# Sixteen of the first block's input products as eight pairs of seven half-size products, in a stretch of their own

## The chip, the cores and the metric

One NeuronCore of a Trainium2 chip (trn2) runs the whole program in one launch. The metric is the device time of that launch in microseconds (us). The engines are TensorE (PE in the rows, its weight loads PEld), VectorE (DVE), ScalarE (ACT), GpSimd (POOL) and the queue of SyncE (SP), which issues most loads.

## The reference, cut to what matters

Two transformer-like blocks run one after the other on 1024 tokens of width 1024. The change is in the first block, where the normalised input (and a context of 256 tokens) is multiplied by one wide matrix and cut into ten parts:

```python
u_l, v_l, q_l, k_l, vv_l, r_l, af_l, ab_l, ga_l, gb_l = jnp.split(h_lat @ w_in, offs, axis=-1)
ql, kl, vl, lfl, lbl = _gla_heads(q_l, k_l, vv_l, af_l, ab_l, w_alpha_f, b_alpha_f, w_alpha_b, b_alpha_b)
o_lf, _ = _gla_scan(ql, kl, vl, lfl, s_cf)
o_lb, _ = _gla_scan(fl(ql), fl(kl), fl(vl), fl(lbl), s_cb)
b_lat = _gla_out(o_lf + fl(o_lb), r_l, gla_norm_g, h_lat.dtype)
a_lat = _chunk_mlp(u_l, v_l, ...)
y = jax.nn.sigmoid(ga) * (a_lat @ w_branch_a) + jax.nn.sigmoid(gb) * (b_lat @ w_branch_b)
```

`u`, `v`, `r`, `ga`, `gb`, `vv` are 1024 wide, `q` and `k` 512. `u` and `r` are needed only after the scan. The rest of the first block, its SwiGLU and the whole second block are untouched.

## The kernel before, in words

**Products.** Every float32 operand is kept as two float32r parts, high and low, and a product is high by high, input low by weight high, and input high by weight low: three matmuls for each of the eight slices of 128 input rows. One weight tile is 128 output columns. A fill job is one tile by 512 tokens, 8 x 3 = 24 matmuls of 128x512 into one PSUM bank (`products_pe`, L319 to L321). A job of kind "rows" (`rows_pe`, L420 to L422) turns it round: 128 tokens are the stationary operand, and the four weight tiles of a group move as 512 columns, so the job needs all four tiles. It waits for the high and low parts of the group's last tile, which are made in order.

**Weights.** `weight_order` lists all tiles. SP loads each tile raw into one of NS = 2 buffers (`weights_sp`, L289; the next load into a buffer waits until the low part of the tile before in it is made), ACT makes the high part (`weights_act`, L271), DVE the low part (`weights_dve`, L278). The parts lie in NW = 4 places (`WH`, `WL`; `place`), and for some tiles in four more (`XWH`, `XWL`, `in_second`), which share memory with `RES`. A high part waits until its place is free (`before_in_place`). When each is made is written into the job that stands at that point of every engine's program: `p.make = n` has ACT and DVE make all tiles below n ahead of what they do for that job, and SP issue loads up to n + 2.

**Stage 1** (`stage1`, about 95 to 320 us) runs 39 jobs: the last tile of `k` (3, one of them the 256 tokens of context), `q` (8), `vv` as rows in two groups of four tiles (20) and half of `v` as rows (8). Beside each job stands one unit of the decays (24 in all: `decay_pe` L904, `decay_act` L919 to L923, `decay_second_dve` L947 to L954) and one dot product for the modulation (32, `mod_dve` L959, with a 512 KB load each).

**Stage 2** (`stage2`, about 320 to 659 us) runs the scan in 20 slots, the two directions in turn, with 40 jobs as fillers, two to a slot: the other half of `v` (8), `u` (16) and `r` (16). A slot is, on PE, two jobs, then the phases 3, 4, 5 of slot n (turn the keys L1263, outputs L1276 and L1278, state L1287), then phase 2 of slot n + 1 (L1251, L1255). DVE, in its program, follows with the states of slot n (L1239), phase 6 (L1191), phase 2 of slot n + 1 (L1209 to L1225) and phase 1 of slot n + 2 (L1197 to L1204), and only then reaches the next job's weights. Steps 0 and 1 of a direction are context slots with no output products, and from step 6 on a slot also adds the other direction's part. The stage's other engines begin when every engine's last signal of stage 1 has come (`gone`).

**Stage 3** (`stage3`, from 659 us) has 32 jobs, `ga` (16) and `gb` (16), with the work on `u`, `v`, `r` and the scan's output behind them (`behind`). Its ACT and DVE programs begin when stage 2 has ended on all engines.

Which engine waits for what around a "rows" job, and where its weights are made, is in these lines:

```python
def fill_act(p):
    if p.make:
        weights_act(p.make)
    ACW.wait_ge(*p.mm)
```

Of the kernel before, what the change touches and what calls it, by code (L numbers as in the profile page):

```python
# [7 lines left out]
F = mybir.dt.float32  # L8
# [7 lines left out]
TC = 256  # L16
NF = 22
EPS = 1e-6
NW = 4
# [44 lines left out]
class Job:  # L64


    def __init__(self, i, name, m, col, n, half, x, ready, bank):
# [7 lines left out]
        self.make, self.group, self.chunk = None, None, None  # L75
# [29 lines left out]
CHUNKS = (8, 12)  # L105

# [19 lines left out]
def program(nc, D, out):  # L126
# [56 lines left out]
    T2H, T2L, T3H, T3L = placed(*(([128, 4, 512], R, n) for n in ("t2h", "t2l", "t3h", "t3l")))  # L183
    XWH, XWL = placed(([128, NW, 1024], R, "xwh"), ([128, NW, 1024], R, "xwl"))
# [53 lines left out]
    def in_second(i):  # L238

        return 5 <= i < 9 or 13 <= i < 17 or 21 <= i < 25  # L240

    def place(i):
        return (i - 1) % NW
# [6 lines left out]

    def before_in_place(i):

        if i < NW or 5 <= i < 9:
            return []
        return [used[i - 2 * NW if 9 <= i < 29 else i - NW]]
# [135 lines left out]
    def plan_rows(jobs, name, group, banks, dst, key, chunks):  # L391

        i = tile_of[(name, 4 * group + 3)]
        for chunk, half, c, x, ready in chunks:
            p = Job(i, name, group, c, 512, half, x, ready, banks[len(jobs) % len(banks)])
            p.bank_free = bank_free[p.bank]
            p.mm = mm.at(more("mm"))
# [5 lines left out]
        for j in range(4):  # L403
            used[i - j] = jobs[-1].mm

    def rows_pe(p):
# [7 lines left out]
        PEW.wait_ge(*w_lo.at(p.i + 1))  # L414
        for k in range(8):
# [96 lines left out]
    def fill_sp(p):  # L512
        if p.make:
            weights_sp(p.make + NS)
# [5 lines left out]
    def stage0():  # L520
# [5 lines left out]
        XC = alloc(p0, [128, 8, TC], F, "xc")  # L526
        mrow = alloc(p0, [2, 2048], F, "mrow")
# [325 lines left out]
    def stage1(parts, xt, low_rank, gone):  # L853

        (al_hi, al_lo, wal_hi, wal_lo, cm_in, cb_silu), done = low_rank
        p1 = ExitStack()
        LG = alloc(p1, [128, 2, 2, 512], F, "lg")
        DG = alloc(p1, [128, 2, 512], F, "dg")
        aw = alloc(p1, [128, 1024], F, "aw")
        aw_in = sig("in", "aw")  # L860
        d_mm, d_abs, d_ln = sig("pe", "decay_product"), sig("ac", "decay_abs"), sig("ac", "decay_log")
# [8 lines left out]
        for group in range(2):  # L870
            plan_rows(jobs, "vv", group, banks, dV, "v", of_context + token_chunks(2, (0, 1)))
        plan_rows(jobs, "v", 0, banks, dVm, "vm", token_chunks(0, (0, 1)))
        for p in jobs:
            p.make = None
        for j, upto in ((0, 7), (2, 8), (3, 9), (5, 10), (7, 11), (8, 12), (9, 13), (11, 14), (13, 15), (15, 16), (17, 17),
# [30 lines left out]
        def pe_():  # L906
            for what, j in steps:
                if what == "fill":
                    fill_pe(jobs[j], None)
                elif j < 24:  # L910
                    decay_pe(j)
# [2901 lines left out]
```

## Time and profile before

| | us |
|---|---|
| median of three runs | 3247.93 (3247.49 to 3249.04) |
| the profiled execution, its own time | 3249.49 |
| its span, first to last instruction | 3248.2 |
| PE busy | 3175.4 (98%) |
| DVE, ACT, POOL busy | 1892.3, 1408.1, 393.3 |
| mean granted TensorE clock | 0.993 |

In a row, the first number is the start or the busy time, and the bracket at the end is the idle time before with what ended it. A matmul's record covers its whole latency, so two records overlap: what a matmul costs in a stream is the distance from one start to the next. A float32 matmul has two records, a float32r matmul one (L1251 issues four float32 matmuls and shows eight records; a fill job issues 24 and shows 24). The granted clock is a share of 2.4 GHz; 0.50 is the lower level, 1.2 GHz.

### The profile page before, as it was taken

The numbers are of one execution on the slowest core, as the hardware profiler recorded it, in microseconds if no ns is written. First come the engines' busy times: TensorE is split into PE (matmuls) and PEld (weight loads), VectorE is DVE, ScalarE is ACT, GpSimd is POOL, SyncE is SP. The second block draws the span as 40 slices with busy tenths as digits, with TensorE's granted clock in tenths as the row PEclk, the third lists the DMA queues.
The fourth block names the chain that finished last, engine by engine and source line by source line (L and its number), as shares of the span: only waits on it lengthen the run. The fifth ranks groups of instructions, "written<-read, shape, count | busy, mean of one in ns | idle before, by whom it ended". The sixth has DMA issues, their size and how long they took to land.

```text
span 3248.2 us, 38749 instructions
## 1 busy us (share of the span) xinstructions
PE 3175.4 (98%) x14558; PEld 2584.2 (80%) x14558; DVE 1892.3 (58%) x3053; ACT 1408.1 (43%) x2336; POOL 393.3 (12%) x625
## 2 busy tenths in 40 slices
PE   6999999999999999999999999999899999999998
PEld 4888788888888878888888887877667888888886
DVE  5562344565334487777444546656686787776443
ACT  4791232254333243333233376575576443333221
POOL 1111000012000200000010200112221200001011
PEclk8999999999999999999999999999999999999999
DMA  5564544456542323334763444355876432336652
GB/s 231 180 223 157 166 149 155 127 209 217 177 143 101 132 98 111 112 115 144 242 197 95 144 136 137 124 172 170 178 114 154 149 123 104 123 104 216 207 189 68
DMA packets 228489, 495.13 MB, mean 152 GB/s; under 512 B 21712, under 2 KB 84816, under 8 KB 226768
## 3 DMA queue, kind: packets, MB, share of 16 engines
q1 hardware_dynamic: 146688, 298.11, 29.2%
q0 software_dynamic: 81616, 194.55, 19.0%
q8 instruction: 117, 1.92, 0.3%
q14 instruction: 68, 0.56, 0.1%
HBM read 353.63 MB, written 138.94 MB: 152 GB/s over the span
## 4 chain that ended last, share of the span: by engine, by line
PE 85%; DVE 7%; ACT 3%; DMA 2%; issue 2%; POOL 0%; SPq 0%; DVEq 0%; POOLq 0%; ACTq 0%
PE p L2273 12%; PE p L2275 12%; PE p L2274 12%; PE p L319 12%; PE p L321 11%; PE p L320 11%; PE p L420 2%; PE p L421 2%; PE p L422 2%; PE p L3341 1%; PE p L1287 1%; PE p L3327 1%; PE p L1276 1%; DMA s_qs<-d_q2l 1%; DMA s_ad<-i_ada 1%
## 5 line engine op out<-in xcount | busy, mean ns | idle before, releaser
L319 PE MATMUL p<-s_xh,s_wh 128*128 128x512 f32 x1936 | 767.1, 396 | 9.8 <-DVE s_tmp L476 6.0
L321 PE MATMUL p<-s_xh,s_wl 128*128 128x512 f32 x1936 | 754.9, 390 | 0.0
L320 PE MATMUL p<-s_xl,s_wh 128*128 128x512 f32 x1936 | 754.3, 390 | 0.0
L2273 PE MATMUL p<-s_xh,s_wh 128*128 128x512 f32 x1152 | 449.7, 390 | 1.5 <-DVE s_wl L2522 1.3
L2275 PE MATMUL p<-s_xh,s_wl 128*128 128x512 f32 x1152 | 448.3, 389 | 0.0
L2274 PE MATMUL p<-s_xl,s_wh 128*128 128x512 f32 x1152 | 448.2, 389 | 0.0
L319 PEld LDWEIGHTS p<-s_xh,s_wh 128*128 128x128 f32 x1936 | 363.6, 188 | 96.6 <-issue 11.1
L321 PEld LDWEIGHTS p<-s_xh,s_wl 128*128 128x128 f32 x1936 | 363.5, 188 | 76.8
L320 PEld LDWEIGHTS p<-s_xl,s_wh 128*128 128x128 f32 x1936 | 363.8, 188 | 74.3 <-issue 1.9
L278 DVE TENSOR_TENSOR s_wl<-s_ws,s_wh 128x1024 fp32r<-128x1024 f32 x143 | 176.7, 1247 | 208.6 <-ACT s_wh L271 208.3
L464 ACT ACTIVATE s_tmp<-p 128x512 f32<-128x512 f32 (+1 forms) x157 | 93.0, 593 | 429.3 <-PE p L321 340.8
L2273 PEld LDWEIGHTS p<-s_xh,s_wh 128*128 128x128 f32 x1152 | 216.2, 188 | 48.8 <-issue 3.6
L2274 PEld LDWEIGHTS p<-s_xl,s_wh 128*128 128x128 f32 x1152 | 216.2, 188 | 45.2 <-issue 0.5
L2275 PEld LDWEIGHTS p<-s_xh,s_wl 128*128 128x128 f32 x1152 | 216.2, 188 | 44.9
L271 ACT ACTIVATE s_wh<-s_ws 128x1024 fp32r<-128x1024 f32 x143 | 148.3, 1050 | 56.0 <-PE p L321 38.6
L2419 ACT ACTIVATE s_wh<-s_ws 128x512 fp32r<-128x512 f32 x148 | 91.9, 625 | 144.5 <-PE p L2275 111.2
L2419 ACT ACTIVATE s_wh<-s_qb 128x512 fp32r<-128x512 f32 x140 | 87.2, 625 | 119.3 <-PE p L2275 109.8
L2643 POOL DMA_DIRECT2D d_h<-s_fhl x80 | 42.6, 533 | 742.7 <-DVE s_fhl L2527 734.3
L2522 DVE TENSOR_TENSOR s_wl<-s_ws,s_wh 128x512 fp32r<-128x512 f32 x148 | 106.3, 731 | 32.6 <-ACT s_wh L2419 32.3
L2522 DVE TENSOR_TENSOR s_wl<-s_qb,s_wh 128x512 fp32r<-128x512 f32 x140 | 100.1, 724 | 40.0 <-ACT s_wh L2419 39.8
L2425 ACT ACTIVATE s_fhl<-s_rb 128x512 fp32r<-128x512 f32 x80 | 50.7, 633 | 151.5 <-DVE s_rb L2567 132.8
L2419 ACT ACTIVATE s_wh<-s_s 128x512 fp32r<-128x512 f32 x80 | 50.0, 625 | 134.7 <-DVE s_s L2512 123.2
(437 smaller groups left out, 5497.4 us busy)
## 6 DMA issues: line engine op xcount, KB each, us to landing
d_h<-s_fhl POOLq DMA_DIRECT2D x80, 512.0 KB, 3.0
s_ws<-i_Wf SPq DMA_DIRECT2D x48, 512.0 KB, 4.2
s_qb<-i_Wf SPq DMA_DIRECT2D x40, 512.0 KB, 4.2
s_qb<-i_Wf SPq DMA_DIRECT2D x80, 256.0 KB, 2.9
s_ws<-i_Wf SPq DMA_DIRECT2D x80, 256.0 KB, 2.8
s_aw<-i_adaT SPq DMA_DIRECT2D x32, 512.0 KB, 3.7
s_xh<-d_h POOLq DMA_DIRECT2D x16, 1024.0 KB, 12.3
s_xl<-d_h POOLq DMA_DIRECT2D x16, 1024.0 KB, 15.4
```

Of the source, the lines that this page charges most:

```text
L271: ac.activation(high_of(i), raw_weights(i)[0], ACT.Copy).then_inc(*w_hi.up())
L278: dv.tensor_tensor(low_of(i), raw_weights(i)[0], high_of(i).bitcast(F), ALU.subtract).then_inc(*w_lo.up())
L319: pe.matmul(o, wh, H[:, k, c:c + n], start=(k == 0), stop=False)
L320: pe.matmul(o, wh, L[:, k, c:c + n], start=False, stop=False)
L321: last = pe.matmul(o, wl, H[:, k, c:c + n], start=False, stop=(k == 7))
L420: pe.matmul(o, xh, wh, start=(k == 0), stop=False)
L464: ac.activation(o, ps, ACT.Copy, scale=p.scale).then_inc(*evA.up())
L2273: pe.matmul(o, wh[:, c], H[:, k, :], start=(start and k == 0), stop=False)
L2274: pe.matmul(o, wh[:, c], L[:, k, :], start=False, stop=False)
L2275: x = pe.matmul(o, wl[:, c], H[:, k, :], start=False, stop=(stop and k == 3))
L2419: ac.activation(half_tile(u.slot)[0], u.src, ACT.Copy).then_inc(*u_hi.up())
L2522: dv.tensor_tensor(l, u.src, h.bitcast(F), ALU.subtract).then_inc(*u_lo.up())
```

## The change

**Seven products in place of eight.** For two weight tiles and all tokens, an output of 256 columns by 1024 tokens over 1024 input rows is cut into halves in all three sizes. Seven half-size products P1 to P7 replace eight. Each is 4 slices x 3 = 12 matmuls of 128x512 (`unit_pe`). Before, such a pair took 4 jobs x 24 = 96 matmuls, now 7 x 12 = 84. It is done for the 8 tiles of `u` and the 8 of `r`: 8 pairs. Four combined inputs are summed once (40 elementwise operations of 128x512, 28 on POOL and 12 on DVE) and split (16 on ACT, 16 on DVE). For each pair, DVE makes four combinations of the raw weights (`fold_dve`) and seven low parts, ACT seven high parts, two copies of one PSUM bank into another as the start of a later sum (`pair_act`, P1 and P6), one copy of P5 into `HELD`, and two outputs; DVE adds `HELD` to the other two. SP loads 1 MB of raw weights per pair, two pairs deep. Two more matmuls, whose result is not used, write the two banks first.

```diff
+SEVEN = ("P1", "P5", "P6", "P2", "P7", "P3", "P4")
+SEVEN_TILES = [(n, m) for n in ("u", "r") for m in range(0, 8, 2)]
+SEVEN_FIRST = 17
...
+        def unit_pe(u, fresh):
...
+            for k in range(4):
...
+                pe.matmul(o, wh[:, c], H[:, k, :], start=(fresh and k == 0), stop=False, skip_group_check=not fresh)
+                pe.matmul(o, wh[:, c], L[:, k, :], start=False, stop=False, skip_group_check=not fresh)
+                x = pe.matmul(o, wl[:, c], H[:, k, :], start=False, stop=(k == 3), skip_group_check=not fresh)
...
+            for u in units:
+                pair_act(pairs[u.n], u.name)
+                high_act(u.i + 7)
+                tail_weights(weights_act, u)
```

**Where it stands.** The 8 pairs are a stretch at the end of stage 1. The order of all other jobs moves: stage 1 has 31 (no `v`), stage 2 has 22 (three tiles of `ga`, 6 jobs, then `v` in two groups of 8), three in slot 0 and one in each later slot, and stage 3 has 26. The places of the weights are renumbered, and only `vv`'s first group still uses `XWH`. The decays' 24 units go in 12 pairs, one every second job, with Abs, Exp and Ln each done for both (`decay_act`). Half the dot products (16) stay beside the jobs and two go with each pair.

```diff
-    for n in ("v", "u", "r", "ga", "gb"):
-        order += [(n, m) for m in range(8)]
+    order += [("ga", m) for m in range(3)] + [("v", m) for m in range(8)]
+    order += [("ga", m) for m in range(3, 8)] + [("gb", m) for m in range(8)]
...
-        return 5 <= i < 9 or 13 <= i < 17 or 21 <= i < 25
+        return 9 <= i < 13
...
-        items = [("u", m, False, "plain", dU, "u", 1.0, TC) for m in range(8)] + [("r", m, False, "plain", dR, "r", 1.0, TC) for m in range(8)]
+        items = [("ga", m, False, "plain", dGA, "ga", 1.0, TC) for m in range(3)]
...
+        plan_rows(jobs, "v", 0, banks, dVm, "vm", token_chunks(0, (0, 1)), (0, 1, 2, 3))
         plan_rows(jobs, "v", 1, banks, dVm, "vm", token_chunks(0, (0, 1)))
-        for j in range(4):
-            jobs[2 * j].make = 26 + j
...
+        for j, upto in ((0, 21), (2, 22), (4, 23), (6, 24), (14, 28)):
+            jobs[j].make = upto
...
-        gaps = [len(jobs) * n // 20 for n in range(21)]
+        gaps = [0] + [len(jobs) - 20 + n for n in range(1, 21)]
```

So tile 23 is the last of `v`'s first group (jobs 6 to 13), and tiles 24 to 27 are its second (jobs 14 to 21); tile 28 is the first of stage 3.

**In pieces.** The last job of `vv`'s second group and of `v`'s first group is done one weight tile at a time, each piece 24 matmuls with 128 moving columns. Each piece signals on its own, and a tile's place counts as used up when its piece is done (`used`):

```diff
+        for a in p.pieces:
+            for k in range(8):
+                xh, xl = H[:, k, p.col:p.col + 128], L[:, k, p.col:p.col + 128]
+                wh, wl = WHg[:, a, k * 128:k * 128 + 128], WLg[:, a, k * 128:k * 128 + 128]
+                pe.matmul(o[:, a, :], xh, wh, start=(k == 0), stop=False)
+                pe.matmul(o[:, a, :], xl, wh, start=False, stop=False)
+                last = pe.matmul(o[:, a, :], xh, wl, start=False, stop=(k == 7))
+            last.then_inc(*mm.up())
```

**Stage 3** drops six filler jobs and its work behind them is drawn together: two `norm` steps behind job 14, the second half's `mix` from 16, `fetch` behind 22 and `first` behind 23.

## Rows read from the trace of the kernel before

**Rows 1.** The page: busy time of the engines, share of the span, instructions.
```profile
PE 3175.4 (98%) x14558; PEld 2584.2 (80%) x14558; DVE 1892.3 (58%) x3053; ACT 1408.1 (43%) x2336; POOL 393.3 (12%) x625
```
**Rows 2.** By stretch: length; busy PE, PEld, DVE, ACT, POOL; granted clock, DMA.
```profile
95.00:320.00 225.00, 225.00 (x1009) 186.80 (x1008) 116.14 (x160) 145.69 (x183) 35.08 (x65) 1.00 0.59 195
...
332.00:338.00 6.00, 4.22 (x11) 3.24 (x12) 2.58 (x6) 0.68 (x3) 0.54 (x1) 0.56 0.70 218
...
382.00:660.00 278.00, 278.00 (x1408) 235.33 (x1407) 127.90 (x257) 75.19 (x135) 21.63 (x40) 1.00 0.44 140
```
**Rows 3.** Timeline of PE, slots 0 and 1 of the scan: start, us.
```profile
327.20 0.39 PE L420 MATMUL p<-s_xwh,s_xh 128*128 128x512 f32 x1
...
330.38 0.39 PE L422 MATMUL p<-s_xwl,s_xh 128*128 128x512 f32 x1
333.09 1.12 PE L1263 MATMUL p<-s_ident,s_ks 128*128 128x128 f32 x4 [2.33 <-DVE s_ks L1211]
...
338.12 0.99 PE L420 MATMUL p<-s_xwh,s_xh 128*128 128x512 f32 x1
...
339.67 0.40 PE L420 MATMUL p<-s_xwh,s_xh 128*128 128x512 f32 x1
...
349.91 0.60 PE L1263 MATMUL p<-s_ident,s_ks 128*128 128x128 f32 x4
...
352.89 0.58 PE L420 MATMUL p<-s_xwh,s_xh 128*128 128x512 f32 x1
```
**Rows 4.** Timeline of PE: float32r with 256 moving columns, first and last of 25.
```profile
105.38 0.28 PE L319 MATMUL p<-s_ch,s_wh 128*128 128x256 f32 x1
...
108.25 0.28 PE L904 MATMUL p<-s_al,s_wal 128*128 128x256 f32 x1
```
**Rows 5.** Timeline of PE: eight records that move one column, each with its load.
```profile
62.72 0.95 PE L641 MATMUL p<-s_ones,s_ad 128*128 128x1 f32 x8
63.52 0.49 PE L319 MATMUL p<-s_xh,s_wh 128*128 128x512 f32 x1
```
**Rows 6.** Timeline of PE where slots 4 and 12 and stage 3 begin.
```profile
382.83 0.50 PE L319 MATMUL p<-s_xh,s_wh 128*128 128x512 f32 x1
...
513.26 1.05 PE L1251 MATMUL p<-s_gq,s_ki 128*128 128x128 f32 x8
514.25 0.68 PE L1255 MATMUL p<-s_gq,s_ks 128*64 128x64 f32 x8
514.86 0.50 PE L319 MATMUL p<-s_xh,s_wh 128*128 128x512 f32 x1
...
658.89 0.58 PE L319 MATMUL p<-s_xh,s_wh 128*128 128x512 f32 x1
```
**Rows 7.** Timeline of DVE at the same three places.
```profile
386.54 0.15 DVE L1204 TENSOR_TENSOR s_ep<-s_eb 128x4 f32<-128x4 f32 x1
...
519.36 1.22 DVE L278 TENSOR_TENSOR s_wl<-s_ws,s_wh 128x1024 fp32r<-128x1024 f32 x1
...
661.51 1.23 DVE L278 TENSOR_TENSOR s_wl<-s_ws,s_wh 128x1024 fp32r<-128x1024 f32 x1 [1.36 <-ACT s_wh L271]
```
**Rows 8.** Timeline of ACT at slot 12 and where stage 3 begins.
```profile
515.58 1.05 ACT L271 ACTIVATE s_wh<-s_ws 128x1024 fp32r<-128x1024 f32 x1
...
660.32 1.06 ACT L271 ACTIVATE s_wh<-s_ws 128x1024 fp32r<-128x1024 f32 x1 [5.58 <-DVE s_S L1239]
```
**Rows 9.** DMA issues, 330 to 660 us: count, KB, median us to landing.
```profile
s_ws<-i_Wr SPq DMA_DIRECT2D x8, 512.0 KB, 3.9
```
**Rows 10.** Groups by line: count | busy us, mean ns of one | idle before.
```profile
L1164 ACT ACTIVATE s_e<-s_gb 128x512 f32<-128x512 f32 x16 | 10.0, 625 | 0.0
...
L2527 DVE TENSOR_TENSOR s_fhl<-s_rb,s_fhl 128x512 fp32r<-128x512 f32 x33 | 22.5, 683 | 0.7 <-ACT s_fhl L2425 0.7
...
L1633 POOL TENSOR_TENSOR s_acc<-s_acc,s_tmp 128x512 f32<-128x512 f32 x49 | 63.8, 1302 | 336.4 <-ACT s_tmp L1626 336.2
...
L959 DVE CUSTOM_DVE_ANT_0 s_aw<-s_aw,s_cb 128x1024 f32<-128x1024 f32 x32 | 39.1, 1222 | 50.1 <-DMA s_aw<-i_adaT 50.1
```

More of the change, by code:

```diff
@@ L396, in plan_rows @@
             p.bank_free = bank_free[p.bank]
+            p.pieces = []
+            if chunk == chunks[-1][0]:
+                p.pieces = pieces
+                for a in pieces[:-1]:
+                    used[i - 3 + a] = mm.at(more("mm"))
             p.mm = mm.at(more("mm"))
@@ L402, in plan_rows @@
             jobs.append(p)
-        for j in range(4):
-            used[i - j] = jobs[-1].mm
+        for a in range(4):
+            if a not in pieces[:-1]:
+                used[i - 3 + a] = jobs[-1].mm
     def rows_pe(p):
@@ L513, in fill_sp @@
         if p.make:
[L514 removed]
+            weights_sp(min(p.make + NS, p.top))
     def ended(*outs):
@@ L879, in stage1 @@
-        steps = beside(len(jobs), [("side", s) for s in range(33)], 1)
-        dbank = [list(bank_free[4]), list(bank_free[5])]
+        decays = [(d, h, part) for d in range(2) for h in range(4) for part in range(3)]
+        steps, n_dots = [], 0
+        for j in range(31):
+            steps += [("before", j), ("fill", j)]
+            if j % 2 == 0 and j <= 24:
+                steps.append(("decay", j // 2))
+            if j % 2 or j == 20:
+                steps.append(("dot", n_dots))
+                n_dots += 1
@@ new lines, in stage1, with load_pair_sp @@
+        dots_of_pair = [list(range(n_dots + 16 * n // n_pairs, n_dots + 16 * (n + 1) // n_pairs)) for n in range(n_pairs)]
+        assert n_dots == 16
+        def load_pair_sp(p):
+            x = RAW[p.n % 2]
+            if p.n >= 2:
+                SPW.wait_ge(*pairs[p.n - 2].units["P4"].lo)
+            elif p.n == 1:
+                SPW.wait_ge(*d_mm.at(24))
+                SPW.wait_ge(*d_scan.at(24))
+                for s in d_out:
+                    SPW.wait_ge(*s.at(12))
+            else:
+                SPW.wait_ge(*w_lo.at(SEVEN_FIRST))
+            for i in range(2):
+                sp.dma_start(x[:, 1024 * i:1024 * i + 1024], D["W" + p.name][p.m + i]).then_inc(*raw[2 * (p.n % 2) + i].up())
@@ L941, in decay_second_dve @@
         def decay_second_dve(u):
-            d, h, part = units[u]
+            d, h, part = decays[u]
             n = parts(True)[part][2]
@@ new lines, in dve_, with store_pool @@
+            for i in range(7):
+                low_dve(i)
+            for u in units:
+                p = pairs[u.n]
+                pair_dve(p, u.name)
+                fold_dve(u.i + 8)
+                low_dve(u.i + 7)
+                if u.name in ("P5", "P2") and dots_of_pair[p.n]:
+                    mod_dve(dots_of_pair[p.n].pop(0))
+                tail_weights(weights_dve, u)
+            mods_end_dve()
+        def store_pool(p, name):
+            o = p.outs[name]
+            POW.wait_ge(*o.ev)
+            dst = dU if p.name == "u" else dR
+            po.dma_start(dst[o.m][:, 512 * o.h:512 * o.h + 512], TMP[:, o.slot, :]).then_inc(*stored[o.slot].up())
@@ L997, in stage1 @@
+            for p in pairs:
+                for name in ("P2", "P7", "P3", "P4"):
+                    store_pool(p, name)
         sp_()
```

398 lines of the change are left out of this document (326 added, 72 removed).

## The prediction

> **What bounds the kernel now.** I read the page first: PE is busy for 3175.4 of 3248.2 us [rows 1], so the sum is first a sum of PE's time. The stretches come next. In those where the change works, PE has no idle time at all in 95 to 320 us and in 382 to 660 us, at the full granted clock, with DVE and ACT about half busy [rows 2]. What ends a wait there is therefore not an average load of DVE or ACT but the moment at which they reach one instruction of their programs. The only stop near the change is in the scan's first slot, where PE waits 2.33 us for DVE [rows 3]. All sums below are against the profiled execution (3249.5 us, its span 3248.2); it stands 1.6 us above the median of the runs, and the forecast is given against that median.
>
> **What is saved.** Fifteen matmuls of 512 columns start from 327.20 to 330.38, 14 distances, so one costs 0.227 us [rows 3]. Eight pairs go from 96 to 84 matmuls: 96 fewer in all, 21.8 us. The two matmuls of no use give back 0.5. Everything else on the list of jobs is only moved: 39 + 40 + 32 = 111 jobs before, 31 + 22 + 26 + 32 after.
>
> **The pieces.** Two jobs of 24 matmuls become two of 96 with 128 moving columns: 48 x 0.227 = 10.9 us go and 192 of an unknown price p come. No float32r matmul in the trace moves 128 columns. With 256 columns the distance is (108.25 - 105.38) / 24 = 0.120 us [rows 4]. When only one column moves behind a load of 128 columns it is (63.52 - 62.72) / 8 = 0.100 [rows 5]: a load with nothing to hide it is no cheaper. So halving the 256 columns can take off little, and 0.100 is the lower end. The upper end is a float32 matmul of 128 columns, which takes two records, (514.25 - 513.26) / 8 x 2 = 0.248 [rows 6]. I take 0.120, because that row has the same number type, the same load and one record. The pieces then cost 23.0 - 10.9 = +12.1 us, with ends at +8.3 and +36.7. What they are for, an earlier free place, can't be used in stage 2: in ACT's program the weights of job 14 stand behind its wait for the whole of job 13.
>
> The Trainium skill, "TensorE: Matmul & The Clock Gate", section Back-to-back issue gap, gives about 81 ns a matmul for sustained streams of 128 columns and about 131 ns for 512. For 512 columns this trace says 0.227, so the section does not fit this kernel; by its 81 ns the pieces would cost 15.6 - 10.9 = +4.7 us as an estimate.
>
> **Waits that the change adds in stage 2.** PE itself keeps up: a slot with one job is 5.4 us + 5.5 of scan, and DVE's chain ends 3.9 us after a job starts (382.83 to 386.69) [rows 6, 7]. The weights don't. A place is free only when the tile four before it has been used, and a "rows" job needs all four tiles.
> - Job 6 needs tile 23, whose place is used until job 5 ends, and whose making is written at job 6. ACT and DVE come to it after their part of slot 3. DVE's part ends at 386.69, and a low part takes 1.22 us [rows 7]: 387.9 against 382.83 [rows 6], PE waits **5.1 us**. Nothing covers it; job 6 is next on PE.
> - Job 14 needs tiles 24 to 27, and all four are made there. The same place in the trace before is slot 12: PE starts its job at 514.86 [rows 6], ACT a high part at 515.58 (1.05 us) [rows 8], DVE a low part at 519.36, so until 520.58 [rows 7]. Two raw tiles are in the buffers, so the second low part is done at 521.8. The third load can be issued only when the first low part is made: 520.6 + 3.9 to land [rows 9] + 1.05 + 1.22 = 526.8. The fourth: 521.8 + 3.9 = 525.7, + 1.05 + 1.22 = 528.0. PE waits **13.2 us**. Behind SP's waits for these loads stand the next slot's loads; they have a slot (12.7 us with job and scan) and are not late.
> - Tile 28 is the first of stage 3, and its place is used until job 21 ends. ACT starts a high part at 660.32, when stage 2 has ended everywhere [rows 8], and DVE's low part ends at 662.74 [rows 7], against PE's 658.89 [rows 6]: **3.9 us**.
> - In slot 0 there are now three jobs ahead of the first turn of keys where there was one and another one: 5.4 us more cover than the 2.33 us wait [rows 3]. That wait goes.
>
> **The clock.** After those 2.33 us idle the granted clock is 0.56 on average from 332 to 338 [rows 2], so mostly the lower level, 1.2 GHz. From the turn of keys to the next fill PE takes 338.12 - 333.09 = 5.03 us, and 352.89 - 349.91 = 2.98 in the next slot; three fills then take 1.55 against 0.68 [rows 3]. A fall so costs 2.9 us. It goes with the wait in slot 0 (-2.3 - 2.9 = -5.2), and comes with the waits of jobs 6 and 14 (+5.8). At stage 3's wait I leave it out and count it in the range.
>
> **What lies beside.** In the seven-product stretch one product is 12 x 0.227 = 2.7 us of PE, a pair 19.1. Per pair ACT has seven high parts and five copies, 12 x 0.625 = 7.5 us, and DVE seven low parts, four sums and two outputs, 13 x 0.683, and two dot products of 1.222, together 11.3 us [rows 10]. Weights are made seven products ahead. The copy that P6 needs has P5's 2.7 us to hide in, and P4's wait for DVE has P3's. All of it counted at nothing; if the chains slip, PE stops once or twice a pair. POOL's 28 sums of 1.302 us are 36 us [rows 10] beside ten jobs of 5.4; they hold stores back by under two jobs, with four buffers. The decays in pairs save ACT some table loads, and nobody waits for ACT there, since PE has no idle time [rows 2]: nothing gained. The first pair's weights: places are freed piece by piece in `vv`'s last job, and there the making does stand ahead of ACT's wait for that job; counted at nothing. Stage 3's tighter list has at most two DVE steps more in one job; nothing, with up to 2 us in the range.
>
> **Sum:** -21.8 + 0.5 + 12.1 - 5.2 + 5.1 + 13.2 + 3.9 + 5.8 = **+13.6 us**. Against the median of 3247.9 that is 3261.5 us. The saving is real, but it is spent on pieces and on weights that come too late.
>
> **Rivals.**
> 1. *Pieces at two records.* If float32r with 128 columns takes what float32 does, +36.7 in place of +12.1: 3286. For it: nothing in this trace runs float32r under 256 columns, and both float32 rows have two records. Against: nothing else makes a float32r matmul take a second record. 0.24.
> 2. *Faster: the weights are in time.* If engines reach the weights of jobs 6, 14 and 28 under cover of the scan, the 22.2 us of waits and 5.8 of clock go: -14.4, 3233.5. Its place is the end of slot 11. It decides once the added waits with their clock are under about 8 us in all, for then the sum is 6.5 us below before. Against: two of the four loads can't be issued before DVE's first low parts, and one load is 3.9 us. 0.09.
> 3. *Cheap pieces.* If loads of a stream overlap further, as in the 64-column row, (514.86 - 514.25) / 8 = 0.076 [rows 6], the pieces cost 14.6 - 10.9 = +3.7 and the kernel takes 3253. Against: that row loads 64 columns, not 128. 0.10. By the 81 ns of "TensorE: Matmul & The Clock Gate" in the Trainium skill it would be 3254, an estimate.
> 4. *The stretch stumbles.* If ACT's copies or DVE's outputs come about 2 us late once a pair, 8 x 2 = 16 us more: 3277. The cover of 2.7 us against a chain of one wait, two ACT instructions and one of DVE (1.9 us) and a dot product behind them speaks for it, DVE's share of 11.3 of 19.1 against. 0.10.
>
> That leaves 0.47 for the forecast. A measurement of this kernel can tell 0.2%, 6.5 us, from no change. Faster is rival 2 and little else: 0.10. Within 0.2% are rival 3 and the forecast with 0.100 a piece and fewer falls of the clock (3252): 0.13. Slower: 0.77. The range goes from 3246 (rival 3 with small gains more) to 3287 (rival 1); outside are rival 2, and rivals 1 and 4 together.
>
> **What would show it.** Twelve matmuls of 128x512 per product at 0.227 us and no PE wait in the stretch; 96 matmuls of 128 columns in each of two jobs, at a distance of 0.12 us (0.25 by rival 1, 0.08 by rival 3); PE idle for about 5, 13 and 4 us, ended by DVE's low part (L278), ahead of job 6, job 14 and stage 3, and none in slot 0; a granted clock of 0.5 behind the first two. I am wrong if PE's idle time in the scan is under 5 us, if the pieces are at 0.2 us or more, or if PE waits in the seven-product stretch.

## The result, and the profile after

The changed kernel takes 3287.07 us (median of 4 runs, 3285.52 to 3287.62) against 3247.71 on the same chip; the ratio is 1.012 with a 95% interval of 1.0102 to 1.0137. It is slower, as forecast, but by 39 us where 13.6 were forecast, and just above the top of the stated range (3287). The profiled execution took 3287.51 us, its span 3286.2. The page's busy line, which answers to [rows 1]:

```profile
PE 3177.2 (97%) x14608; PEld 2588.0 (79%) x14608; DVE 1984.7 (60%) x3169; ACT 1404.9 (43%) x2376; POOL 438.9 (13%) x653
```

PE is busy for 1.8 us more than before in a span that is 38.0 us longer: nearly all that came is time in which PE stands still. The waits of PE from 90 to 900 us say where (waiting line, releasing line; total us, times, longest us). L445 is the first matmul of a `rows` job, L1100 of a half-size product, L328 of a plain job, L287 and L1274 are DVE's low parts:

```profile
PE p L445 <- DVE s_wl L287: 18.8, 2, 13.8
PE p L1100 <- DVE s_wl L1274: 11.9, 1, 11.9
PE p L445 <- DVE s_xwl L287: 4.6, 1, 4.6
PE p L328 <- DVE s_wl L287: 3.6, 1, 3.6
PE p L1633 <- ACT s_kt L1519: 3.0, 4, 0.7
PE p L328 <- ACT s_tmp L489: 0.9, 1, 0.9
```

The first row holds the waits of jobs 6 and 14, the fourth that of stage 3's entry, all three forecast. The second and the third, 16.5 us, were not: at the entry of the seven-product stretch, and at job 11 of stage 1, the first of `vv`. Both in PE's timeline, with the first and the last of the 96 matmuls of `vv`'s pieces between them, and the end of the stretch (L328 at 455.49 follows its last product):

```profile
169.19 0.77 PE L445 MATMUL p<-s_xwh,s_ch 128*128 128x512 f32 x1 [4.59 <-DVE s_xwl L287]
...
277.95 0.22 PE L434 MATMUL p<-s_wh,s_xh 128*128 128x128 f32 x1
...
288.50 0.28 PE L436 MATMUL p<-s_wl,s_xh 128*128 128x128 f32 x1
...
301.25 0.77 PE L1100 MATMUL p<-s_xh,s_wh 128*128 128x512 f32 x1 [11.95 <-DVE s_wl L1274]
...
455.49 0.39 PE L328 MATMUL p<-s_xh,s_wh 128*128 128x512 f32 x1
```

From 277.95 to 288.50 there are 95 distances between matmuls of 128 columns, 0.111 us each.

Behind each of the five waits (job 11, the entry, jobs 6 and 14 at 508.8 and 618.5, stage 3) the granted clock is at its lower level, 1.2 GHz, for a few us. By stretch (length; busy PE, PEld, DVE, ACT, POOL with instructions; granted clock, DMA):

```profile
169.00:176.00 7.00, 6.81 (x17) 5.39 (x18) 0.69 (x2) 0.00 (x0) 0.63 (x2) 0.55 0.70 225
...
301.20:305.00 3.80, 3.75 (x9) 3.00 (x10) 3.80 (x7) 0.00 (x0) 0.00 (x0) 0.50 0.12 44
...
508.80:514.00 5.20, 5.14 (x14) 4.07 (x15) 0.00 (x0) 0.00 (x0) 0.00 (x0) 0.57 0.69 202
...
618.50:623.00 4.50, 4.50 (x12) 3.54 (x13) 0.00 (x0) 0.00 (x0) 0.00 (x0) 0.55 0.87 257
...
724.80:729.00 4.20, 4.17 (x11) 3.32 (x12) 1.02 (x1) 0.00 (x0) 0.00 (x0) 0.59 1.00 413
```

Busy time less matmuls times 0.227 is what each fall costs: 6.81 - 17 x 0.227 = 2.95, then 1.7, 2.0, 1.8 and 1.7, in all 10.1 us, where the kernel before had one fall of 2.9 in this part.

One instruction behind the whole change makes a good mark, since the code after it is the same in both kernels: the first matmul with `s_ones` and `s_acc`, where stage 3 has ended. Before and after (minimum/median/maximum ns, first and last start):

```profile
L1648 PE MATMUL p<-s_ones,s_acc x64: 164/250/372, 1103.1 to 3236.4; 128*128 128x1 f32 x64
```
```profile
L1994 PE MATMUL p<-s_ones,s_acc x64: 164/250/271, 1138.1 to 3274.5; 128*128 128x1 f32 x64
```

It comes 35.0 us later, and 3.1 us more arise behind it (2136.4 against 2133.3 us from first to last start). Below, "at the mark" means this first start. The account up to the mark: -21.8 + 0.5 + 10.4 (pieces as measured, 192 x 0.111 - 10.9) - 5.2, that is -16.1; waits 4.6 + 11.9 + 5.0 + 13.8 + 3.6 + 0.9 = +39.8; the clock +10.1: +33.8 of 35.0 us. Without its waits the change does save 16 us; the waits and the clock behind them cost 50.

**Why the stretch starts late.** DVE's timeline shows what the waits alone don't. These are sums and low parts of the combined inputs, then a dot product:

```profile
255.24 1.78 DVE L957 TENSOR_TENSOR s_e1f<-s_xh 128x512 f32<-128x512 f32 x1
257.05 1.67 DVE L959 TENSOR_TENSOR s_e1f<-s_e1f,s_xl 128x512 f32<-128x512 f32 x1
...
276.74 7.27 DVE L973 TENSOR_TENSOR s_e1l<-s_e1f,s_e1h 128x512 fp32r<-128x512 f32 x4
...
287.44 2.30 DVE L1239 CUSTOM_DVE_ANT_0 s_aw<-s_aw,s_cb 128x1024 f32<-128x1024 f32 x1
...
291.94 2.48 DVE L973 TENSOR_TENSOR s_t2l<-s_t2f,s_t2h 128x512 fp32r<-128x512 f32 x4
...
300.43 0.68 DVE L1274 TENSOR_TENSOR s_wl<-s_ws,s_wh 128x512 fp32r<-128x512 f32 x1
```

Most operations of 128x512 with two inputs take 1.67 to 1.8 us each where one took 0.68 in the kernel before [rows 10], and the dot product 2.30 against 1.22. At 291.94 the same operation is back at 0.62 each (2.48 for four). What ended just then stands in POOL's timeline:

```profile
288.74 2.12 POOL L952 TENSOR_TENSOR s_e4f<-s_e4f,s_xl 128x512 f32<-128x512 f32 x1
290.81 1.62 POOL L532 DMA_DIRECT2D d_v<-s_tmp  x3
```

While POOL sums, DVE's operations take 2.5 times as long, and POOL's own take up to 2.24 us (at 240.94) where such a sum took 1.30 before [rows 10]. From 250.5 us to the entry DVE has no idle time, so it is late by the length of its operations and not by a wait for POOL's sums. The Trainium skill, "GPSIMD Engine Reference", section 1. Specifications, says that GpSimd's SBUF interfaces are shared with VectorE, with contention for VectorE instructions that have two SBUF inputs; the trace agrees, and gives the size: 1.7 against 0.68 us. DVE so arrives late at its last item before the stretch, the low part of the first product (300.43 us), and PE, done at 289.3, waits for it.

Two explanations were open: the contention itself, or the **order** in which ACT and DVE take the weights' parts and the combined inputs (the first parts stand behind inputs that only the seventh product needs). At the late makes of stage 2 and at `vv`, an order was suspected too.

### The profile page after: what moved, and what is told of

It reads as the page before. It is cut to its first block, busy times and chain, and to the rows that moved or that the text cites. A ratio compares the mean times of both kernels' runs of the same rounds, so it can differ in the third digit from the quotient of the medians.

```text
span 3286.2 us, 39106 instructions
## 1 busy us (share of the span) xinstructions
PE 3177.2 (97%) x14608; PEld 2588.0 (79%) x14608; DVE 1984.7 (60%) x3169; ACT 1404.9 (43%) x2376; POOL 438.9 (13%) x653
## 4 chain that ended last, share of the span: by engine, by line
PE 78%; DVE 10%; ACT 5%; issue 4%; DMA 3%; POOL 1%; SPq 0%; DVEq 0%; ACTq 0%; POOLq 0%
PE p L2619 12%; PE p L2621 12%; PE p L2620 12%; PE p L328 9%; PE p L330 9%; PE p L329 9%; PE p L1100 2%; PE p L1101 2%; PE p L1102 2%; PE p L3687 1%; PE p L1633 1%; PE p L445 1%; PE p L446 1%; PE p L447 1%; PE p L3673 1%
## 5 line engine op out<-in xcount | busy, mean ns | idle before, releaser
L328 PE MATMUL p<-s_xh,s_wh 128*128 128x512 f32 x1744 | 694.8, 398 | 13.9 <-DVE s_tmp L501 5.5
L330 PE MATMUL p<-s_xh,s_wl 128*128 128x512 f32 x1744 | 682.6, 391 | 0.0
L329 PE MATMUL p<-s_xl,s_wh 128*128 128x512 f32 x1744 | 682.5, 391 | 0.0
L2619 PE MATMUL p<-s_xh,s_wh 128*128 128x512 f32 x1152 | 449.6, 390 | 1.5 <-DVE s_wl L2868 1.3
L2621 PE MATMUL p<-s_xh,s_wl 128*128 128x512 f32 x1152 | 448.3, 389 | 0.0
L2620 PE MATMUL p<-s_xl,s_wh 128*128 128x512 f32 x1152 | 448.2, 389 | 0.0
L328 PEld LDWEIGHTS p<-s_xh,s_wh 128*128 128x128 f32 x1744 | 329.6, 189 | 93.3 <-issue 15.1
L330 PEld LDWEIGHTS p<-s_xh,s_wl 128*128 128x128 f32 x1744 | 329.5, 189 | 70.1
L329 PEld LDWEIGHTS p<-s_xl,s_wh 128*128 128x128 f32 x1744 | 330.0, 189 | 67.7 <-issue 1.9
L287 DVE TENSOR_TENSOR s_wl<-s_ws,s_wh 128x1024 fp32r<-128x1024 f32 x135 | 166.8, 1249 | 237.8 <-ACT s_wh L280 237.6
L2619 PEld LDWEIGHTS p<-s_xh,s_wh 128*128 128x128 f32 x1152 | 216.3, 188 | 48.2 <-issue 3.6
L2620 PEld LDWEIGHTS p<-s_xl,s_wh 128*128 128x128 f32 x1152 | 216.3, 188 | 45.4 <-issue 0.5
L2621 PEld LDWEIGHTS p<-s_xh,s_wl 128*128 128x128 f32 x1152 | 216.3, 188 | 44.8
L489 ACT ACTIVATE s_tmp<-p 128x512 f32<-128x512 f32 (+1 forms) x125 | 73.4, 589 | 276.4 <-PE p L330 170.5
L280 ACT ACTIVATE s_wh<-s_ws 128x1024 fp32r<-128x1024 f32 x135 | 139.6, 1050 | 74.4 <-PE p L330 37.3
L2868 DVE TENSOR_TENSOR s_wl<-s_qb,s_wh 128x512 fp32r<-128x512 f32 x140 | 100.0, 724 | 39.9 <-ACT s_wh L2765 39.8
L1979 POOL TENSOR_TENSOR s_acc<-s_acc,s_tmp 128x512 f32<-128x512 f32 x49 | 63.8, 1303 | 337.3 <-ACT s_tmp L1972 337.1
## 6 DMA issues: line engine op xcount, KB each, us to landing
s_xl<-d_h POOLq DMA_DIRECT2D x16, 1024.0 KB, 14.7
```

The source lines that it names most:

```text
L280: ac.activation(high_of(i), raw_weights(i)[0], ACT.Copy).then_inc(*w_hi.up())
L287: dv.tensor_tensor(low_of(i), raw_weights(i)[0], high_of(i).bitcast(F), ALU.subtract).then_inc(*w_lo.up())
L328: pe.matmul(o, wh, H[:, k, c:c + n], start=(k == 0), stop=False)
L329: pe.matmul(o, wh, L[:, k, c:c + n], start=False, stop=False)
L330: last = pe.matmul(o, wl, H[:, k, c:c + n], start=False, stop=(k == 7))
L489: ac.activation(o, ps, ACT.Copy, scale=p.scale).then_inc(*evA.up())
```

## The experiments

Times are medians; "before" is the kernel before, run beside it on the same chip: 3247.86 for the first four, 3247.82 for the next four, 3248.59 for the next four, then 3250.36 and 3247.2. Line numbers are those of each kernel. Each edit is made on the changed kernel unless it says otherwise. The bracket behind a ratio is its 95% interval: about 5 us either way for the first six runs, 3 us for the others. So a difference of 2 or 3 us between two of these kernels is not shown by their times; where it matters, the mark of the two profiles is given too.

**POOL's sums, 32 columns.** The 28 sums are cut from 512 to 32 columns, and the inputs that they made are read from the plain input instead. So three of the four combined inputs, and with them `u` and `r`, are not computed; every instruction count stays.

```diff
-            po.tensor_tensor(T2F[:, k, :], T3F[:, k, :], h11, ALU.add)
+            n = slice(0, 32)
+            po.tensor_tensor(T2F[:, k, n], T3F[:, k, n], h11[:, n], ALU.add)
```

> POOL's 28 sums for the combined inputs do 32 columns in place of 512, and the combined inputs 2, 3 and 4 are read from the plain input, so u and r are not computed rightly; instructions, waits and their order stay. If DVE is late at the entry of the seven-product stretch because its two-input operations and POOL's slow each other, the DVE sums of E1 (now 1.7 us each) fall to 0.69 us, PE's wait at the entry falls from 11.9 us to under 3, and the time by 11 to 13 us, to about 3275. If DVE is late by its own list of instructions alone, they keep their 1.7 us or the wait stays above 8 us, and the time falls by less than 4.

Measured: 3272.35 us, 14.7 less than the changed kernel; ratio to before 1.0075 (1.0059 to 1.009). DVE's timeline and PE's waits:

```profile
250.84 0.69 DVE L963 TENSOR_TENSOR s_e1f<-s_e1f,s_xl 128x512 f32<-128x512 f32 x1
...
259.12 1.39 DVE L977 TENSOR_TENSOR s_e1l<-s_e1f,s_e1h 128x512 fp32r<-128x512 f32 x2
```
```profile
PE p L445 <- DVE s_wl L287: 18.8, 2, 13.7
PE p L445 <- DVE s_xwl L287: 4.7, 1, 4.7
```

DVE's operations are at 0.69 us, and the wait at the entry is gone altogether, 11.9 us and its clock; nothing else moved. That the contention takes the time at the entry is shown. Whether it must cost time is not: another order could still hide it.

**Stage 2's weights earlier.** Tiles 23 and 27 are made a job earlier, and 28 at job 21.

```diff
-        for j, upto in ((0, 21), (2, 22), (4, 23), (6, 24), (14, 28)):
+        for j, upto in ((0, 21), (2, 22), (4, 23), (5, 24), (13, 28), (21, 29)):
```

> Only the jobs at which weights are made in stage 2 change: tile 23 at job 5 in place of 6, tiles 24 to 27 at job 13 in place of 14, tile 28 at job 21. If the waits ahead of job 6 (5.0 us), job 14 (13.8) and stage 3 (3.6) come from where the making stands in ACT's and DVE's programs, the first and third vanish, the second becomes about 3 us inside slot 11, and with the clock falls the time is 22 to 28 us less: about 3262. If they come from the places and buffers themselves, the waits move to other instructions of the same slots and the time falls by under 10.

Measured: 3261.78 us, 25.3 less; ratio 1.0041 (1.0027 to 1.0056). PE's waits:

```profile
PE p L1100 <- DVE s_wl L1274: 12.6, 1, 12.6
PE p L1633 <- ACT s_kt L1519: 4.8, 5, 1.7
PE p L445 <- DVE s_xwl L287: 4.6, 1, 4.6
```

The three waits (22.4 us) and the clock behind them (5.5 by the stretches above) are gone; 1.8 us came back at ACT's copy of the keys and 0.7 at the entry, which makes 25.4. Three table entries cost the kernel 25 us: those waits were a matter of the place in ACT's and DVE's programs, not of load.

**`v`'s first group whole**, without pieces (the last argument of its `plan_rows` call is dropped).

```diff
-        plan_rows(jobs, "v", 0, banks, dVm, "vm", token_chunks(0, (0, 1)), (0, 1, 2, 3))
+        plan_rows(jobs, "v", 0, banks, dVm, "vm", token_chunks(0, (0, 1)))
```

> The last job of v's first group is done whole, with 24 matmuls of 512 columns. If its pieces buy nothing, since ACT's weights of job 14 stand behind its wait for the whole job, the time falls by what the pieces cost, 96 x 0.110 - 24 x 0.227 = 5.1 us, to 3282. If they let weights be made earlier, PE's wait ahead of job 14 grows from 13.8 and the time falls by under 2 us or rises.

Measured: 3281.8 us, 5.3 less, ratio 1.0101 (1.0084 to 1.0118); job 14 waits 13.9 us as before. The price of one job in pieces by the measured distance is 96 x 0.111 - 24 x 0.227 = 5.2. So close an agreement is partly luck: the four runs spread from 3279.4 to 3285.1, and the profiled one, the slowest, is only 2.0 us ahead at the mark (1136.1), since its lower clock behind job 14 lasts 6.1 us against 4.0 and the waits at the entry and at job 11 are 1.0 us longer. That the wait at job 14 stays is what the run shows.

**`vv`'s last job whole** (the same argument dropped in its call).

> The last job of vv's second group is done whole. If DVE's backlog sets when the seven-product stretch begins, PE gets there 5.1 us earlier and waits about 17 us in place of 11.9, and the time is the same within 2 us. If the wait is only for weights of places set free by the pieces, the time falls by about 5 us; if the pieces pay for themselves it rises by 3 or more.

Measured: 3286.53 us, ratio 1.0119 (1.0104 to 1.0134), no change. PE is done about 5 us earlier and waits about as much longer:

```profile
PE p L1100 <- DVE s_wl L1274: 17.3, 1, 17.3
```

DVE alone sets the start of the stretch.

**`vv`'s tile 12 earlier.**

```diff
-        for j, upto in (... (6, 11), (8, 12), (9, 13), (12, 14), ...
+        for j, upto in (... (6, 11), (8, 13), (12, 14), ...
```

> The weights of vv's first group of four (tile 12) are made one job earlier, ahead of a pair of decays, nothing else is changed. Theory (the engines take the tile's two parts behind a pair of decays, whose chain through ScalarE and VectorE is now twice as long): the wait of 4.6 us at job 11 of stage 1 falls under 1 us and the low clock after it goes, so 3287 - 4.6 - 2 to 3 = about 3280 (3278 to 3282), as long as the entry of the seven-product stretch stays at its 11.9 us. Rival (the raw weight rows come late, or the chain of decays as a whole is behind): less than 2 us of the wait goes, 3285 to 3287. A third case: the wait goes and the entry grows by the same amount, because VectorE's backlog sets the entry and not PE's place; then the wait at L1100 grows to 15 to 19 us and the time stays at 3285 to 3288.

Measured: 3278.72 us, 8.4 less, ratio 1.0093 (1.0078 to 1.0108). No wait for `s_xwl` is left, and that of the entry is 10.8. In the changed kernel ACT's timeline had shown the tile's high part behind a pair of decays:

```profile
161.68 0.47 ACT L1138 ACTIVATE s_lg<-p,s_vec 128x256 f32<-128x256 f32 x1 [1.16 <-DVE s_dg L1232]
...
164.42 1.28 ACT L1146 ACT_TABLE_LOAD   x1
165.72 1.12 ACT L1146 ACTIVATE s_lg<-s_lg,s_ones 128x512 f32<-128x512 f32 x2
166.74 1.04 ACT L280 ACTIVATE s_xwh<-s_ws 128x1024 fp32r<-128x1024 f32 x1
```

It starts at 166.74, but PE had been free from 164.6 on. Pairs halve the table loads but make each chain longer: 6.9 us of ACT's time go by from the pair's start at 159.84 to the tile's part, where one unit's chain in the kernel before takes 4.6 (154.35 to 158.91). The run shows that the tile's place behind the chain costs the time. That the pair's length is what made it late is read from these two timelines; no run undoes the pairs.

**A first other order at the entry.** The parts of the first two tiles ahead of the last inputs, on ACT and DVE.

```diff
                 if what == "before" and j == 30:
                     for i in range(6):
                         high_act(i)
+                    for t, k in hi_order[12:16]:
+                        combined_act(t, k)
...
+                    fold_dve(1)
+                    for i in (0, 1):
+                        low_dve(i)
+                    for t, k in lo_order[8:12]:
+                        combined_dve(t, k)
```

> On ScalarE and VectorE the parts of the first two weight tiles of the seven-product stretch stand ahead of the last combined inputs (t2 and t4), which the stretch needs only some units later. Theory A (position: the weights are ready late because they stand behind sums that wait for GpSimd): the wait at L1100 falls from 11.9 us to 0 to 4, the low clock after it shrinks, time 3272 to 3278. Theory B (VectorE's slow two-input operations beside GpSimd are the bound, wherever they stand): the wait falls by under 4 us, or comes back inside the stretch as waits for t2 and t4, time 3283 to 3288. Halfway (both): a wait of 5 to 8, time 3278 to 3283.

Measured: 3289.76 us, ratio 1.0126 (1.0111 to 1.0141): 2.7 more, which is within the intervals. PE's waits at the stretch:

```profile
PE p L1100 <- ACT s_wh L1154: 8.2, 1, 8.2
...
PE p L1100 <- ACT p L1168: 3.8, 1, 3.8
```

The total stays at 12.0: 8.2 ahead of the first product and a new one for ACT's copy of the first product, which this order puts behind the parts of `t4`. By time this is nearest to theory B, and the first wait did fall by under 4 us (3.7). But the second one is not for the inputs `t2` or `t4`, as B has it, so the run leaves the question open.

**The three orders at once:** stage 2, tile 12 and this entry.

> The earlier makes of stage 2, the earlier tile of vv and the reordered entry at once. If the waits are independent of each other, as the account of the trace has it: 3287 - 25.3 (measured for the makes alone) - 7 - 12 = about 3243 (3238 to 3250), the gain of the change without its waits. If vv's wait and the entry share one backlog of VectorE: the 7 us come back at the entry, 3248 to 3254. If the contention binds at the entry: 3255 to 3262.

Measured: 3251.65 us, ratio 1.0009 (0.9999 to 1.0018); the waits at the entry are 7.0 and 2.8. The time lies in the second forecast (3248 to 3254), but that forecast's mechanism, `vv`'s 7 us coming back at the entry, is not seen: 9.8 us of waits stand there against 12.0. It is 35.4 us under the changed kernel; the runs alone gave 25.3 + 8.4 - 2.7 = 31.0, so within the noise the orders don't take from each other. What is missing to the first forecast is the entry, which this order did not mend.

**The same with `vv`'s last job whole.**

> As the run with all three orders, and vv's last job whole, without the pieces by output tile. Theory (the pieces hide no wait once the makes are in time, and vv's last 64 pieces cost 64 x 0.110 - 16 x 0.227 = 3.4 us more than the whole job): 2 to 5 us under the run with all three. Rival (PE then reaches the entry sooner and waits there as long as it saved): the same time within 1 us. If the context slots do need the output tiles apart: 1 to 5 us over it.

(The expectation miscounts: the job in pieces has 96 matmuls, whole it has 24, and the difference is 5.2 us.) Measured: 3253.57 us, ratio 1.0017 (1.0007 to 1.0027). By the medians this is 1.9 more, by the marks 1.9 less (1102.8 against 1104.7), so no change is shown. The wait at the entry is 11.9 in place of 7.0 and took back 4.9 of the 5.2 us, as for the job alone.

**A second order.** Added to stage 2's and tile 12's: the first product's low part and the second's sums directly behind the first inputs, `t2`'s parts ahead of `t3`'s, the copy of the first product ahead of later parts.

```diff
-        lo_order = [(t, k) for t in (1, 3, 2, 4) for k in range(4)]
+        lo_order = [(t, k) for t in (1, 2, 3, 4) for k in range(4)]
...
+                elif what == "before" and j == 29:
+                    low_dve(0)
+                    fold_dve(1)
+            low_dve(1)
+            for t, k in lo_order[4:8]:
+                combined_dve(t, k)
```

> As the run with all three orders (3251.7), with another order at the entry. Its trace shows where the first trial of an order failed: the low part of the first unit stands on VectorE at 287.8 us, behind the sums of the second unit and behind the low parts of t3 (5.9 us beside GpSimd's sums, needed only by the fifth unit) and two dots, and the copy of the first product stands on ScalarE behind four high parts of t4 and two parts that wait for VectorE. Here the first unit's low part and the second unit's sums stand ahead of t3's parts, t2's ahead of t3's, and the copy ahead of the fifth unit's parts. Theory (position in two queues): the waits of 7.0 and 2.8 us at the entry fall to 0 to 2 together and the low clock goes with them, 3251.7 - 9 - 2 = about 3240 (3237 to 3244), under the kernel before. Rival (VectorE has too much work before the entry, whatever the order): waits of 6 us or more stay, 3247 to 3252.

Measured: 3248.57 us, ratio 0.9999 (0.999 to 1.0008), level with the kernel before and 4.6 us above the upper end that the theory gave. PE goes into the stretch without a wait, and stops once, ahead of the fifth product:

```profile
PE p L1100 <- ACT p L1178: 5.9, 1, 5.9
```

**Two dots moved** from jobs 27 and 29 into the stretch (`if (j % 2 and j < 27) or j == 20`).

> As the run before it, and the two dots of jobs 27 and 29 moved into the seven-product stretch. Theory (order alone was the cause): within 1 us of the run with the new order. Rival (VectorE's backlog still counts): 2 to 5 us less than that run, the wait at the entry shorter by up to the 3.5 us that the two dots take.

Measured: 3248.78 us, ratio 0.9997 (0.9988 to 1.0006), the same time as without the move. That does not show that the load counts for nothing: the wait at L1178 fell from 5.9 to 4.6 us, and the fifth product starts 1.7 us earlier (297.35 against 299.08). All of it was lost at the end of the stretch, where stage 2's first jobs wait longer for ACT's copy. In the run before and in this one:

```profile
455.30 0.50 PE L328 MATMUL p<-s_xh,s_wh 128*128 128x512 f32 x1 [0.90 <-ACT s_tmp L489]
```
```profile
455.52 0.50 PE L328 MATMUL p<-s_xh,s_wh 128*128 128x512 f32 x1 [2.45 <-ACT s_tmp L489]
```

ACT stands there behind the load of `s_gb`, which landed at about the same time in both, and a fall of the clock followed (0.61 from 455.5 to 459). So DVE's load has a share of 1.3 us or more in the wait at the fifth product, and the equal time is a gain that the next wait took.

**The last job of `v`'s first group whole, too.**

> As the run with the dots moved, and v's first job whole. Theory (the pieces hide no wait once the weights are in time): 96 x 0.110 - 24 x 0.227 = 5.1 us less (4 to 6 less), as in the run where this was undone alone (5.3 less). Rival (the pieces stand in for the wait of 2.3 us that the kernel before had in this slot): only 1 to 3 us less.

Measured: 3253.63 us, ratio 1.0018 (1.0009 to 1.0027): **4.9 more** (2.9 at the mark), where alone it had given 5.3 less (2.0). PE waits 7.5 us for ACT's copy of the keys at 585.8 us. ACT's timeline here, and then in the run before it:

```profile
582.17 1.06 ACT L280 ACTIVATE s_wh<-s_ws 128x1024 fp32r<-128x1024 f32 x1 [3.91 <-DMA s_ws<-i_Wv]
583.75 1.06 ACT L280 ACTIVATE s_wh<-s_ws 128x1024 fp32r<-128x1024 f32 x1 [0.51 <-DMA s_ws<-i_Wv]
584.71 0.58 ACT L489 ACTIVATE s_tmp<-p 128x512 f32<-128x512 f32 x1
585.18 0.59 ACT L1532 ACTIVATE s_kt<-p 128x512 f32<-128x512 f32 x1
```
```profile
583.40 1.06 ACT L280 ACTIVATE s_wh<-s_ws 128x1024 fp32r<-128x1024 f32 x1 [1.00 <-DMA s_ws<-i_Wv]
584.37 0.58 ACT L489 ACTIVATE s_tmp<-p 128x512 f32<-128x512 f32 x1
584.84 0.59 ACT L1532 ACTIVATE s_kt<-p 128x512 f32<-128x512 f32 x1
```

With the makes a job earlier, ACT's four high parts stand ahead of the copy and wait for raw rows; ACT is done with it at nearly the same time in both (0.35 us apart). A shorter job only brings PE there sooner, and the wait brings a fall of the clock with it (granted clock 0.50 from 586 to 590 us); the next job starts at 591.44 against 588.91. Those 2.5 us are the loss that the traces show; the rest of the 4.9 is not accounted for. So with the weights made a job earlier these pieces cost nothing: they stand where PE would wait.

**Both jobs whole.**

> As the run before it, and vv's last job whole too. Theory (there is now nothing behind PE's place at the entry): 3 to 5 us less again. Rival (as in the two runs where this was undone before: PE comes to the entry earlier and waits there as long as it saved): the same time within 1.5 us, with a wait at L1100 that is 3 to 5 us longer.

Measured: 3255.59 us, ratio 1.0022 (1.0013 to 1.0031), 2.0 more than the run before it, within the intervals; beside 5.4 at L1178 (5.3 before) there are further waits at L1100 of 2.1, 1.3 and 0.9 us. The rival had it: nothing saved, and the waits in the stretch 4 to 5 us longer, though in several pieces.

**The copies first,** on top of the second order: ACT takes high parts 4 to 11 only behind the copies of the first pair's products.

```diff
-                for i in (4, 5, 6, 7) if u.i == 0 else (u.i + 7,):
+                for i in {0: (), 1: (4,), 2: (5, 6, 7), 3: (8,), 4: (9, 10, 11)}.get(u.i, (u.i + 7,)):
```

> As the run with the new order at the entry (3248.6), and on ScalarE the copies of the first pair's products stand ahead of the parts of later units. In that run the first four units ran without a wait, and one wait of 5.9 us stood ahead of the fifth (L1100 on ScalarE's L1178): the copy of the third product stood behind a part whose sum VectorE makes only at 295 us. Theory (order in the queues alone): that wait falls under 1.5 us and no low clock follows, 3248.6 - 5 - 2 = 3241 to 3244, under the kernel before by 0.15 to 0.25%. Rival (VectorE cannot make the first two pairs' parts in time): the wait comes back ahead of the fifth to ninth unit, 4 us or more, 3246 to 3249.

Measured: 3249.62 us, ratio 1.0 (0.9991 to 1.0009). The theory's 3241 to 3244 is missed, and the rival's place and size came true (4 us or more ahead of the fifth to the ninth product). The wait at L1178 is gone, and one has come ahead of the seventh product:

```profile
307.04 0.79 PE L1100 MATMUL p<-s_e4h,s_wh 128*128 128x512 f32 x1 [7.92 <-DVE s_tmp L1286]
```

Its releaser in DVE's timeline stands behind a dot product that waits for a DMA:

```profile
305.14 1.23 DVE L1241 CUSTOM_DVE_ANT_0 s_aw<-s_aw,s_cb 128x1024 f32<-128x1024 f32 x1 [1.91 <-DMA s_aw<-i_adaT]
...
306.30 0.69 DVE L1286 TENSOR_TENSOR s_tmp<-p,s_held 128x512 f32<-128x512 f32 x1
```

**The same with the two dots moved.**

> The same with the two dots of jobs 27 and 29 moved into the seven-product stretch. Theory: within 1 us of the run with the copies first. Rival (VectorE's backlog counts once the copies are in time): 2 to 4 us less than it.

Measured: 3250.27 us, ratio 1.0002 (0.9993 to 1.0011), the same time again; the wait at L1286 is 6.8 in place of 7.9, and that for ACT's copy at the end of the stretch 2.6 in place of 0.9, as in the other run with the dots moved.

**The first pair's output sums first,** on top of the copies: DVE adds them ahead of later parts, its dots behind.

```diff
+            pair_dve(pairs[0], "P7")
             for u in units:
                 p = pairs[u.n]
-                pair_dve(p, u.name)
+                if p.n:
+                    pair_dve(p, u.name)
+                if u.i == 2:
+                    pair_dve(p, "P3")
...
-                if u.name in ("P5", "P2") and dots_of_pair[p.n]:
+                if u.name in (("P5", "P2") if p.n else ("P7", "P3")) and dots_of_pair[p.n]:
```

> As the run with the copies first (3249.6), and on VectorE the first pair's two output sums stand ahead of the parts of later units and the pair's two dots behind them. In that run PE was fed without a wait up to the sixth unit and then waited 7.9 us for VectorE's L1286, which stood behind a dot whose rows (a DMA) landed only at 305.1 us. Theory (order in the queues alone; at each reordering the wait has moved to the next misplaced instruction): no wait over 3 us is left in the seven-product stretch and no low clock there, 3249.6 - 6 - 2 = 3240 to 3243, under the kernel before by 0.2%. Rival (the stretch's first pair asks VectorE for more than it has): 4 us or more of waits come back at the second pair, 3246 to 3250.

Measured: 3244.57 us, ratio 0.9993 (0.9984 to 1.0002), 42.5 under the changed kernel (41 by the ratios) and the lowest of all, 1.6 above the theory's range. Its interval still holds the kernel before, so no gain over that one is shown. PE's waits up to 1200 us, and the mark:

```profile
PE p L1650 <- ACT s_kt L1536: 4.4, 5, 1.7
PE p L1100 <- DVE s_tmp L1286: 2.2, 1, 2.2
PE p L1100 <- ACT p L1178: 1.7, 1, 1.7
```
```profile
L2011 PE MATMUL p<-s_ones,s_acc x64: 164/250/372, 1094.6 to 3231.4; 128*128 128x1 f32 x64
```

Both L1100 waits stand in the second pair (at 314.15 us ahead of its fifth product, at 322.10 ahead of its seventh), 3.9 us in all. The theory's "no wait over 3 us" holds, but the rival's place is met too, and its "4 us or more" nearly. So the work on ACT and DVE around the first pair may still reach into the next.

At the mark it is 8.5 us ahead of the kernel before. By the steps, -16.1 + 2.2 + 1.7 + 1.5 (copies of keys, 4.4 against the 2.9 of the kernel before) make -10.7, so 2.2 us are not accounted for. Over the three orders at once (mark at 1104.7) the three reorderings inside the stretch gave 10.1 us by the marks, 7.1 by the medians and 5 by the ratios. That settles the entry: with all of POOL's sums in place, PE enters the stretch without a wait. DVE's slow operations take the time, and the order let PE wait for them there; taking away either one ends the wait at the entry. Behind it, the 3.9 us in the second pair stay open between order and load.

## Why the prediction was right and wrong

**Right:**
- *Saving*, 96 matmuls at 0.227. The stretch runs from 301.25 to 455.49: 154.2 us, less 1.7 of low clock, over 672 matmuls is 0.227. There is no PE wait inside it, so rival 4 did not come. For the first pair that was partly luck: the 11.9 us at the entry gave ACT and DVE a lead. Once that wait was gone, PE stopped inside the first pair (5.9 us ahead of the fifth product, later 7.9 ahead of the seventh), as the prediction's "if the chains slip" has it, and in the last run still 3.9 us in the second. From the third pair on no run has a wait in the stretch.
- *Jobs 6 and 14, stage 3.* 5.1, 13.2 (its own terms give 13.1) and 3.9 us forecast; 5.0, 13.8 and 3.6 measured, ended by DVE's low part as said. The run with the makes earlier took away just this. Rival 2, that they are in time, needed that edit.
- *Slot 0.* Its wait of 2.33 us is gone.
- *Pieces.* 0.111 us each against 0.120: +10.4 for +12.1. They take one record each, so rival 1 fell, though its 3286 is next to the measured time: a number met for the wrong reason. Rival 3's 0.076 fell too, and so did the 81 ns of the Trainium skill's "TensorE: Matmul & The Clock Gate", section Back-to-back issue gap.
- *The clock* cost 2.0 and 1.8 behind jobs 6 and 14 against 2.9 each.

**Wrong:** the step that failed is the counting of what lies beside PE. Three things were put at nothing, two of them in the part "What lies beside".
1. *"POOL's 28 sums of 1.302 us are 36 us [rows 10] beside ten jobs of 5.4".* I asked whether POOL was done in time and who waits for POOL, and not what its work does to DVE's. With the first pair's weights, "counted at nothing" too, this cost 11.9 us and 1.7 of clock; the run with small sums gave back 14.7. The argument offered as cover was the freed places. These were free in time; the engine that had to fill them was not.
2. *"The decays in pairs ... nobody waits for ACT there ...: nothing gained."* I looked for a gain only. One tile fell behind the longer chain: 4.6 us and 3.0 of clock; moving the tile gave 8.4.
3. *The clock at stage 3*, left out of the sum and put into the range: 1.7.

These are 22.9 us. With the pieces 1.7 and the clock at two jobs 2.0 lower than forecast, and 1.1 more in waits, 13.6 becomes the account's 33.8 (33.9 by rounded terms), against 35.0 at the mark. The last 3 us lie in unchanged code and need no cause in the change: from the mark's first to its last start the profiles of these kernels take between 2132.7 and 2138.0 us.

## What to carry to other kernels

- Work given to an idle engine must be asked two questions: is it done in time, and whose work does it slow. Here 28 sums on POOL made DVE's two-input operations 2.5 times as long while they ran.
- An engine that is half busy can still be late at one instruction. Where work gets faster on PE, list what each new first consumer needs and what stands ahead of it in the other programs: three entries of a table were worth 25 us.
- A wait removed by a new order can go to the next misplaced instruction, so an unchanged time does not say that the edit did nothing: see where the waits stand now. Here it went from the first product to the fifth to the seventh at 10, 6 and 8 us, and then shrank to 4. And an edit measured while another wait binds can change its sign: the whole job gave -5.3 us and later +4.9. Moving two dot products shortened one wait by 1.3 us and lengthened a later one by 1.6, and the time was the same.

## What was not expected of the hardware

- DVE and POOL slow each other while both do two-input operations on SBUF: mostly 1.67 to 1.8 us for 0.68 on DVE, and up to 2.24 for 1.30 on POOL. Dot products of 1024 columns took 2.3 for 1.2. Operations on 32 columns on POOL left DVE at 0.69.
- A float32r matmul of 128 columns with its own load takes 0.111 us, hardly less than 0.120 for 256 columns; 512 take 0.227.
- The lower clock followed each of the five PE waits of 3.6 us or more, and cost 1.7 to 3.0 us each. A wait so costs 1.1 to 1.6 times what the view of waits shows. The falls up to the mark are 10.1 us in the changed kernel and 2.9 in the kernel before.
